# Nine odd merge gates in a stage of their own: eight of them as pairs, one alone; the four quarters of the state put together by VectorE

## What is computed

```python
u = rms_norm(x) @ w_in                                   # 8192 columns and 3 * 1024 gates
ya, yb, yc = three attentions of 512 columns each, each times its own SiLU gate
gates = sigmoid(mg).reshape(b, s, 3, D_MODEL)
m = gates[:, :, 0] * (ya @ wa) + gates[:, :, 1] * (yb @ wb) + gates[:, :, 2] * (yc @ wc)
x = x + rms_norm(m @ w_out, post_g)
x = x + sigmoid(x @ w_pg) * (p_i @ w_pe)
```

## Time and profile before

| what | value |
|---|---|
| median of 3 runs (lowest, highest) | 1332.03 us (1331.99, 1332.58) |
| profiled execution, first to last instruction (its span) | 1330.3 us |
| TensorE busy in it | 1312.1 us, 99% |
| VectorE, ScalarE, GpSimd busy | 680.8, 575.5, 352.0 us |
| granted clock of TensorE, mean | 1.000 |

### The profile page before, as it was taken

The page is one execution under the profiler, slowest core; times in us unless marked ns, Lnnn a source line. Parts: engine busy times, 40 slices in busy tenths (PEclk is TensorE's granted clock), DMA queues, the critical chain, the costliest instruction groups (busy, mean ns, idle before and its releaser), DMA issues.

```text
span 1330.3 us, 17488 instructions
## 1 busy us (share of the span) xinstructions
PE 1312.1 (99%) x6636; PEld 1072.0 (81%) x6636; DVE 680.8 (51%) x1285; ACT 575.5 (43%) x1106; POOL 352.0 (26%) x239
## 2 busy tenths in 40 slices
PE   8999999999999999999999999999999999999998
PEld 6788877888888778788888888888877888888887
DVE  6354655556522677786633435555557337435222
ACT  6355455553222577676422245555554223223210
POOL 4122212222434311130244512221211443213100
PEclk9999999999999999999999999999999999999999
DMA  6111112111111200000111211111001114422111
GB/s 214 63 41 41 46 36 57 52 32 52 49 48 32 67 30 16 17 20 21 52 52 32 81 61 33 51 51 42 32 24 41 48 40 167 140 81 70 58 40 40
DMA packets 25712, 72.18 MB, mean 54 GB/s; under 512 B 2808, under 2 KB 4728, under 8 KB 25504
## 3 DMA queue, kind: packets, MB, share of 16 engines
q1 hardware_dynamic: 25632, 71.09, 16.9%
HBM read 66.86 MB, written 4.23 MB: 53 GB/s over the span
## 4 chain that ended last, share of the span: by engine, by line
PE 90%; DVE 4%; ACT 3%; issue 1%; DMA 1%; POOL 1%; SPq 0%; ACTq 0%; DVEq 0%; POOLq 0%
PE ps L934 18%; PE ps L953 14%; PE ps L1290 13%; PE ps L1548 7%; PE ps L1528 6%; PE ps L1175 5%; PE ps L1342 5%; PE ps L1331 2%; PE ps L973 2%; PE ps L1112 2%; PE ps L1028 2%; PE ps L1260 2%; PE ps L1554 2%; PE ps L1406 2%; PE ps L1143 1%; PE ps L1234 1%
## 5 line engine op out<-in xcount | busy, mean ns | idle before, releaser
L728 POOL TENSOR_TENSOR w_lo<-stage,w_hi 128x1024 fp32r<-128x1024 f32 (+2 forms) x84 | 190.3, 2265 | 577.5 <-ACT w_hi L1598 577.5
L1598 ACT CAST w_hi<-stage 128x1024 fp32r<-128x1024 f32 (+2 forms) x92 | 91.3, 992 | 198.0 <-PE ps L934 125.9
L2148 DVE TENSOR_TENSOR pt_lo<-ps,pt_hi 128x512 fp32r<-128x512 f32 (+2 forms) x160 | 97.1, 607 | 80.6 <-ACT pt_hi L1962 40.3
L953 PE MATMUL ps<-h_hi,w_hi 128*128 128x512 f32 x272 | 110.3, 405 | 0.0
L934 PE MATMUL ps<-h_hi,w_hi 128*128 128x512 f32 x352 | 108.9, 391 | 0.7 <-POOL w_lo L728 0.7
L934 PE MATMUL ps<-h_lo,w_hi 128*128 128x512 f32 x352 | 108.5, 389 | 0.0
L934 PE MATMUL ps<-h_hi,w_lo 128*128 128x512 f32 x352 | 108.4, 389 | 0.0
L1290 PE MATMUL ps<-h_hi,w_hi 128*128 128x512 f32 x256 | 106.8, 417 | 0.0
L953 PE MATMUL ps<-h_hi,w_lo 128*128 128x512 f32 x272 | 106.2, 391 | 0.0
L953 PE MATMUL ps<-h_lo,w_hi 128*128 128x512 f32 x272 | 106.1, 390 | 0.0
L1290 PE MATMUL ps<-h_hi,w_lo 128*128 128x512 f32 x256 | 100.5, 392 | 0.0
(11 more groups left out here) (386 smaller groups left out, 3059.3 us busy)
## 6 DMA issues: line engine op xcount, KB each, us to landing
stage<-in_w_gates SPq DMA_DIRECT2D x24, 512.0 KB, 3.6
stage<-in_w_qkvg_a SPq DMA_DIRECT2D x19, 512.0 KB, 4.4
stage<-in_w_qkvg_c SPq DMA_DIRECT2D x16, 512.0 KB, 3.6
m<-in_x_tok SPq DMA_DIRECT2D x8, 512.0 KB, 6.4
stage<-in_w_branch SPq DMA_DIRECT2D x8, 512.0 KB, 3.7
y_plain<-in_x_tok SPq DMA_DIRECT2D x8, 512.0 KB, 3.7
stage<-in_w_pg SPq DMA_DIRECT2D x16, 256.0 KB, 3.0
out<-y_plain SPq DMA_DIRECT2D x16, 256.0 KB, 2.0
```

Of the source, the lines that this page charges most:

```text
L728: nc.gpsimd.tensor_tensor(dst, stage[:, staged, 0:width], f32(hi), ALU.subtract).then_inc(w_ready, 1)
L953: done = mm(ps[:, half_bank(T), :], w[:, slot, k * P:(k + 1) * P], h[:, k, g * SEQ:(g + 1) * SEQ], start=k == 0 and part == 0, stop=k == K ...
L1598: nc.scalar.copy(dst, stage[:, staged, 0:width]).then_inc(w_hi_done, 1)
L2148: sub = lambda out, whole, hi: nc.vector.tensor_tensor(out, whole, f32(hi), ALU.subtract)
```

## The change

The nine gate blocks (0,3), (0,5), (0,7), (1,3), (1,5), (1,7), (2,3), (2,5), (2,7), written (branch, f), leave the merges. A new stage stands between the first q and k products and attention A. In it (0,3) is multiplied plainly (`plain_gate`, 24 matmuls for each group, the first of them ahead of q and k of group 1) and the other eight as four pairs: with 1024 features in, each of the 7 products is 4 chunks x 3 = 12 matmuls (`gate_product`). The state is here h itself. VectorE puts four quarters of it together (`whole`, hi plus lo, 2048 columns a partition), forms four sums of quarters, and ScalarE and VectorE split them again. VectorE also sums and splits the quarters of the weights, pair by pair, and adds the products up; ScalarE takes tanh of each quarter, and SyncE stores it to a scratch tensor in DRAM (18 stores of 256 KB). In the merges, gate rows 3, 5 and 7 are loaded back from there into `s_row(1)` (9 loads of 512 KB), and TensorE's order is branch 0, branch 1, gate 2, then pairs and single gates in turn. In merge 2 both gates 4 and 6 stand behind pair 1, and pair 2 is followed at once by branch 6. The first six blocks of w_out are loaded earlier, ahead of branch 6's weights, and rounded by ScalarE between its splits. SyncE's wait for `merged` to be complete stands newly ahead of the loads of x for the output stage. The lambda sums on VectorE move behind the new stage.

The constants and, on SyncE, a gate row's load:

```diff
-N_MERGE = [19, 42, 74]
+N_MERGE = [19, 39, 68]
+MERGE_LOADS = [[0, 1, 2, 3, 4, 5, 7, 8, 10, 11]] * 2 + [[0, 1, 2, 3, 4, 5, 7, 8, 9, 11, 12]]
...
+GATE_PLAIN = (0, 3)
+GATE_PAIRS = [((0, 5), (0, 7)), ((1, 3), (1, 5)), ((1, 7), (2, 3)), ((2, 5), (2, 7))]
...
+            def load_gate_row(b, f):
+
+                sp.wait_ge(merged, LEAD + b * KC + f - 1)
+                sp.dma_start(s_row(1), gate_scratch[b * KC + f]).then_inc(row_in[1], 16)
```

TensorE in the merges:

```diff
             def merge_rest(b):
...
-                merge_gate(b, 2, n + 3, 1 - slot, 0)
-                merge_branch(b, 1, n + 4, slot)
-                merge_gate(b, 3, n + 5, 1 - slot, 1)
...
+                merge_branch(b, 1, n + 3, (n + 1) % 2)
+                merge_gate(b, 2, n + 4, n % 2, 0)
                 for p in PAIRS[b]:
...
-                    pair_first(b, p, n + 4 * p + 2, slot)
-                    if last:
-                        pair_rest(b, p, n + 15, 1 - slot)
-                    else:
-                        merge_gate(b, 2 * p + 2, n + 4 * p + 3, 1 - slot, 0)
-                        pair_rest(b, p, n + 4 * p + 4, slot)
-                        merge_gate(b, 2 * p + 3, n + 4 * p + 5, 1 - slot, 1)
+                    pair_first(b, p, at, at % 2)
+                    pair_rest(b, p, at + 1, 1 - at % 2)
+                    for c, number in enumerate(gates_behind(b, p)):
+                        merge_gate(b, 2 * p + 2 + 2 * c, number, number % 2, c)
                 if KC // 2 - 1 not in PAIRS[b]:
-                    merge_branch(b, 6, n + 14, slot)
-                    merge_branch(b, 7, n + 15, 1 - slot)
+                    merge_branch(b, 6, n + 11, (n + 11) % 2)
+                    merge_branch(b, 7, n + 12, (n + 12) % 2, count=2)
```

TensorE at the start (`gate_product` waits in `gw_ready` for a weight's rest and in `gt_ready` for a state's):

```diff
+            def gate_product(J, product):
...
+                gate_bank_free(7 * J + product)
+                if product == P1:
+                    pe.wait_ge(gw_ready, 4 * J + 2)
+                elif product == P3:
+                    pe.wait_ge(gw_ready, 4 * J + 3)
+                elif product == P7:
+                    pe.wait_ge(gw_ready, 4 * J + 4)
+                if J == 0 and product >= P6:
+                    pe.wait_ge(gt_ready, T_LO.index(state) + 1)
+                for c in range(QT):
+                    cols = slice(first + c * P, first + (c + 1) * P)
...
             first_product("k", 0, range(5, KC))
+            plain_gate(0)
             first_product("q", 1, range(KC))
             first_product("k", 1, range(KC))
+            plain_gate(1)
+            for J in range(N_PAIRS):
+                for product in range(7):
+                    gate_product(J, product)
+            pe.wait_ge(g_added, 7 * N_PAIRS - 4)
             half_step(-2, lambda T: None)
+            pe.wait_ge(g_tanh, GROUPS + 4 * N_PAIRS)
             score_pair(0)
```

VectorE at the start:

```diff
+            def whole(T, half, g):
+                hi, lo = h_quarter(half, g)
+                nc.vector.tensor_tensor(G_SUM[T], f32(hi), f32(lo), ALU.add).then_inc(gt_whole, 1)
...
             first_lo("q", 0)
+            dve.wait_ge(h_ready, LEAD + TILES)
+            whole(1, 0, 0)
+            whole(3, 0, 1)
+            whole(2, 1, 1)
+            first_lo("k", 0)
+            whole(4, 1, 0)
+            gate_a22_lo(0)
...
+            gate_a1_lo(0)
+            gate_state_sums()
+            gate_w_sums(0)
+            first_lo("q", 1)
+            gate_state_lo(2)
+            gate_sum_lo(0, 0)
...
+            for J in range(N_PAIRS):
+                gate_adds(J)
```

More of the change, by code:

```diff
@@ L608, in _ @@
             sp.wait_ge(f_stored, 16)
-            for c in range(2):
-                sp.sem_inc(o_stored[c], LEAD)
             def load_raw(i):
@@ new lines, in gate_product @@
+            def gate_product(J, product):
+                a, a22 = G_A1, G_A22[J % 2]
+                (s2s4, s3s1) = G_S
+                (hi, lo), first, state = {P1: (a, 0, "11"), P2: (a, SEQ, "21"), P3: (s2s4, SEQ, "22"), P6: (s2s4, 0, 2),
+                                          P7: (s3s1, 0, 3), P5: (s3s1, SEQ, 1), P4: (a22, 0, 4)}[product]
+                gate_bank_free(7 * J + product)
+                if product == P1:
+                    pe.wait_ge(gw_ready, 4 * J + 2)
[7 more added lines that the diff above has]
+                    cols = slice(first + c * P, first + (c + 1) * P)
+                    for part, (w, h) in enumerate([(hi, 0), (hi, 1), (lo, 0)]):
+                        done = mm(ps[:, g_bank(J, product), :], w[:, cols], G_STATE[state][h][:, c, :],
+                                  start=c == 0 and part == 0, stop=c == QT - 1 and part == 2)
+                done.then_inc(g_done, 1)
@@ L1597, in split_w @@
                     dst = w_hi[:, slot, 0:width]
-                nc.scalar.copy(dst, stage[:, staged, 0:width]).then_inc(w_hi_done, 1)
+                nc.scalar.copy(dst, stage[:, staged, 0:width]).then_inc(w_hi_done, count)
             def to_hi(dst, bank, scale, signal):
@@ L1818, in merge_tanh, with merge, split @@
                 nc.scalar.activation(s_row(c), banks(gate_bank(b, c)), ACT.Tanh, scale=0.5).then_inc(mg_tanh, 1)
-            def merge(b):
-                n, slot = N_MERGE[b], N_MERGE[b] % 2
-                uses = lambda k: (n + k) // 2 + 1
+            def merge(b, beside=None):
+                n = N_MERGE[b]
+                def split(number, width=TOK, staged_as=None, count=1):
+                    staged, uses = merge_staged(b, number if staged_as is None else staged_as)
+                    split_w(number, number % 2, uses, width=width, staged=staged, count=count)
                 def pair(p):
-                    number, last = pair_number(b, p), p == KC // 2 - 1
-                    raw_w = stage[:, slot, :]
-                    split_w(n + 4 * p + 2, slot, uses(4 * p + 2))
+                    number, at = pair_number(b, p), pair_at(b, p)
+                    slot = at % 2
+                    staged, _ = merge_staged(b, at)
+                    split(at)
                     if p == 1:
@@ new lines, in merge, with plain_gate_hi @@
+                    split(n + 11, width=512)
+                    beside(range(2, 4))
+                    split(n + 12, width=512, count=2)
+                    act.wait_ge(block_done, LEAD + n + 9)
+                    act.wait_ge(merged, LEAD + b * KC + 5)
+                    nc.scalar.activation(s_row(0), banks(gate_bank(b, 1)), ACT.Tanh, scale=0.5).then_inc(mg_tanh, 1)
+            def plain_gate_hi():
+                act.wait_ge(gp_in, 16)
+                nc.scalar.copy(G_PLAIN[0], stage[:, 0, :]).then_inc(gw_hi_done, 1)
@@ L1904, in _ @@
             square_x(7)
+            plain_gate_hi()
             for t in range(5, TILES):
@@ L2432, in _ @@
+            first_lo("k", 1)
+            gate_state_lo(3)
+            gate_sum_lo(0, 1)
+            gate_state_lo(1)
+            gate_state_lo(4)
+            for J in range(N_PAIRS):
+                gate_adds(J)
             dve.wait_ge(const_in, 16 * 3)
```

532 lines of the change are left out of this document (387 added, 145 removed).

## The result

The changed kernel took 1335.77 us in the median of 7 runs (1334.34 to 1337.96), the kernel before 1332.43 in as many: a ratio of 1.0027 with a 95% interval of 1.0018 to 1.0037, 3.3 us slower. It lies in the range (1326.5 to 1338.5), on the slow side of the forecast 1333.2. The profiled execution has a span of 1334.0 us, 3.7 above the one before.

What follows compares the result with a forecast made beforehand. TensorE's count of matmuls was taken as the bound (busy 1312.1 of 1330.3 us). Terms -10.9 - 0.4 - 0.3 + 1.3 + 3.1 + 6.3 + 2.1 = +1.2 gave 1333.2 us, range 1326.5 to 1338.5.

Steps and rivals of the forecast that it cites:

- Matmuls, -10.9: TensorE: nine gate blocks of 432 matmuls become 384, 48 fewer at 0.2267 us each, -10.9 us.
- The start, -0.4: Ahead of q of group 1: the first plain gate fills TensorE's 0.40 us wait, -0.4 us.
- P3, +1.3: Gate stage, first pair's third product: waits for VectorE's rest of the first weight sum, +1.3 us (0.6 to 2.5).
- Pair 1 in merges 1 and 2, +3.1: Pair 1 waits for GpSimd's and VectorE's chains without a gate ahead: 1.2 in merge 1, 1.9 in merge 2.
- Merge 0 and the other pairs, 0: Merges: merge 0 has its state ready early, other pairs' gates are split in time; no cost, 0 us.
- Branch 6, +6.3: Merge 2: branch 6 waits for VectorE's sums of pair 2, no longer covered by gate 7, +6.3 us (6.2 to 7.2).
- Rival 4: Merge 2: no wait at branch 6, its banks being freed earlier; 1324.8 us, chance 0.10.
- The clock, +2.1: Behind the branch 6 wait in merge 2: TensorE's clock falls after the idle time, +2.1 us (0 to 2.1).
- Rival 1: Merge 2: the clock stays up in the wait at branch 6; 1331.1 us, chance 0.20.
- Rival 2: Gate stage and merges: neither the first pair's third product nor first pairs wait, clock stays; 1326.7 us, chance 0.12.
- Rival 3: Tight chains of gate stage and merges: VectorE and GpSimd collide in full, 2.1 us each; 1338.3 us, chance 0.16.
- The forecast of no difference beyond what can be measured: Whole kernel: the change stays within some 0.2% (2.7 us) of the kernel before; chance 0.51.

Runs made afterwards that it cites:

- The version with nearly all the waits removed: Changed kernel plus four order edits, branches in the gates' banks, GpSimd's late block 5 rest, two w_out rests in VectorE's idle time: 1321.76 us (0.9919).
- the repetition: The changed kernel itself, unaltered, timed again in the second set beside the kernel before: 1335.5 us (1.0022).
- the experiment that kept it busy: Changed kernel plus 24 matmuls without use in the wait ahead of branch 6 of merge 2: 1332.96 us (1.0005).

## Why the prediction was right, and by how much it was off

- **Matmuls, -10.9.** Right. The version with nearly all the waits removed is 10.6 (8.8 to 12.7) below the kernel before.
- **The start, -0.4.** The gap went, as said, 0.6 with its restart. The 0.6 us by which the first q product came later were not in the forecast and are no part of the change: it began between 18.86 and 20.95 us in the thirteen traces of versions that are alike up to there, as the first weights landed (the expectation of the repetition has the third and fourth tile of x; ScalarE's wait ahead of the rounding of the weights says otherwise). The latest, 20.95, has a stretch of lower clock ahead of it as well. The earlier trace rows was one draw.
- **P3, +1.3.** It cost 1.4 with the restart. The chain of VectorE was laid out as it ran, with one collision in it: two of its operations took 5.22 us beside a copy of 1.73 on GpSimd, some 0.7 more than alone. That a mere change of order takes the wait away was not seen.
- **Pair 1 in merges 1 and 2, +3.1.** The mechanism was right, the term was too small: 4.4 with the wait at attention C's start, 0.1 longer than before. The step that failed is the size of GpSimd's three operations, 5.8 us with up to 1.3 more for a collision, of which I took only a part. In merge 1 they took 7.1 (714.86 to 721.94), the first 3.03 instead of 2.40 and the last 1.79 instead of 1.17, since VectorE's rests and its addition of branch 1 now ran beside them, and in merge 2 6.5. And the price of a restart was left out, 0.24 for each wait, 0.5 for the two waits of each merge. Behind this chain stood a second, VectorE's addition of branch 1, which the forecast did not name.
- **Merge 0 and the other pairs, 0.** Merge 0's own pairs did not wait, and neither did gates 4 and 6. But attention B's start did, 0.56 us idle and 0.8 in all. The step that failed is "the last pairs of merges 0 and 1 were without gates before": true, but in merge 0 the 8 transposes stood ahead of the last pair, and the change moves them. I priced the gates that move and not the transposes.
- **Branch 6, +6.3.** 6.2 idle, 6.4 with the restart. VectorE's chain took 12.9 us from the first sum (1099.79) to the last (1112.69) with the wait for products, and GpSimd did not disturb it, as laid out. Rival 4 fell: in the banks that the change gives it, the branch must wait. In other banks it need not, which I had not looked for.
- **The clock, +2.1.** The fall was there, with 2.4 and 1.8 us lost in two traces of the same kernel; the granted clock is at its lower level at 1112.7 and back before 1117.8. Rival 1 fell. The Trainium skill's "TensorE: Matmul & The Clock Gate", Part 1, which says that an idle array falls to half of its clock until it has been busy for a time, is borne out by this trace, and by the experiment that kept it busy.
- **Rival 2** (the chains hold) fell with the three waits. **Rival 3** (VectorE and GpSimd collide in full) did not come in the changed kernel, whose tight chains lost 1.4 us more than laid out (5.8 for 4.4), not 5.1. Full collisions were there, one of VectorE's rests ahead of pair 1 in each of merges 1 and 2 took 3.42 and 3.43 us for 1.22, but on VectorE's chain, which ended 0.6 us ahead of GpSimd's. The rival's price came in an experiment that put two more operations on GpSimd.

The forecast of no difference beyond what can be measured was not met, narrowly (1.0027 against 1.002). The trace lies 2.5 us above the forecast sum: pair 1 gave 1.3 of it, the start of attention B 0.8, the later first q product 0.6 and the clock 0.3, and the gap at the start and the output tile took 0.6 back. The terms are of one sign for the most part because I took waits at their idle time and one place at nothing; the 0.6 of the start is chance.
